# One core, expert stage of a two-block layer: the last 128 tokens' expert rows fetched by indirect DMA and multiplied on VectorE, TensorE's products 384 tokens wide

## The reference

```
def peer_ffn(h, w_q, sub_keys, u, v):        # blocks of 128 tokens, 8 heads, 128 keys, top 16
    q = (hx @ w_q).reshape(TOKEN_BLOCK, PEER_HEADS, 2, PEER_HALF)
    s = jnp.einsum('nhpd,hpkd->nhpk', q, sub_keys)
    ...                                      # top 16 of each half, top 16 of their 256 sums
    expert = (i1 * N_KEYS + i2).reshape(TOKEN_BLOCK, PEER_HEADS * PEER_TOPK)
    gate = jax.nn.softmax(best_s, axis=-1)
    u_sel = u[expert]                        # [128 tokens, 128 experts, 1024]
    v_sel = v[expert]
    act = jax.nn.gelu(jnp.einsum('nd,ned->ne', hx, u_sel), approximate=False)
    return jnp.einsum('ne,ned->nd', gate * act, v_sel)
```

## Time and profile before

| | us |
|---|---|
| three timed runs | 2605.48, 2605.72, 2604.08; median 2605.48 |
| profiled execution | 2603.68, its span 2601.9 |
| TensorE busy | 2467.9 (95%), 12856 matmuls |
| GpSimd busy | 1559.2 (60%) |
| VectorE busy | 1405.7 (54%) |
| ScalarE busy | 585.3 (22%) |
| DMA | 375.41 MB, mean 144 GB/s |
| matmuls of the experts and other weights from `hT` / of the down product (line 683) | 1055.8 / 667.4 busy |

### The profile page before, as it was taken

The page is one execution under the profiler, slowest core; times in us unless marked ns, Lnnn a source line. Parts: engine busy times, 40 slices in busy tenths (PEclk is TensorE's granted clock), DMA queues, the critical chain, the costliest instruction groups (busy, mean ns, idle before and its releaser), DMA issues.

```text
span 2601.9 us, 37796 instructions
## 1 busy us (share of the span) xinstructions
PE 2467.9 (95%) x12856; PEld 1258.8 (48%) x12856; DVE 1405.7 (54%) x2431; ACT 585.3 (22%) x1194; POOL 1559.2 (60%) x1048
## 2 busy tenths in 40 slices
PE   6879989999999999999999999999899898999997
PEld 3435534444555555434444444444357544457743
DVE  6996748998677777229722222240204533564434
ACT  2112211111222222111111111110126332245412
POOL 6764459888766766799866666560570166830063
PEclk8989999999999999999999999999999999999999
DMA  6224443555447857877755655560220022210021
GB/s 261 92 79 156 142 164 122 149 154 150 141 147 237 257 153 238 264 258 269 247 203 200 206 198 208 198 217 13 82 97 1 9 89 89 97 49 1 9 73 49
DMA packets 189247, 375.41 MB, mean 144 GB/s; under 512 B 13536, under 2 KB 79200, under 8 KB 189152
## 3 DMA queue, kind: packets, MB, share of 16 engines
q1 hardware_dynamic: 119696, 332.64, 38.2%
q10 hardware_dynamic: 69456, 41.50, 5.4%
HBM read 302.78 MB, written 71.30 MB: 144 GB/s over the span
## 4 chain that ended last, share of the span: by engine, by line
PE 83%; POOL 2%; DVE 2%; issue 1%; ACT 1%; DMA 0%; DVEq 0%; SPq 0%; POOLq 0%; ACTq 0%
PE ps L683 68%; PE ps L820 4%; PE ps L841 4%; PE ps L829 2%; PE ps L953 2%; PE ps L764 1%; POOL arena L653 1%; POOL parts L635 1%; DVE ps L1337 1%; ACT arena L1091 0%; POOL ring L633 0%; POOL arena L651 0%; DVE arena L1370 0%; PE ps L812 0%; PE ps L1053 0%
## 5 line engine op out<-in xcount | busy, mean ns | idle before, releaser
L683 PE MATMUL ps<-hT,parts 128*128 128x512 f16 x4800 | 1055.8, 380 | 38.2 <-DVE arena L1371 14.1
L632 POOL TENSOR_SCALAR parts<-ring 128x1024 f16<-128x1024 f32 x261 | 289.0, 1107 | 809.4 <-PE ps L683 784.1
L683 PEld LDWEIGHTS ps<-hT,parts 128*128 128x128 f16 x4800 | 467.0, 98 | 597.7 <-issue 22.3
L683 PE MATMUL ps<-arena 128*128 128x512 f16 x3072 | 667.4, 380 | 6.7 <-DVE arena L1734 6.7
L635 POOL TENSOR_TENSOR parts<-ring,parts 128x1024 f16<-128x1024 f32 x261 | 568.8, 2179 | 21.8
L683 PEld LDWEIGHTS ps<-arena 128*128 128x128 f16 x3072 | 301.2, 98 | 373.7 <-issue 14.8
L1729 DVE TENSOR_TENSOR arena<-arena 128x512 f32<-128x512 f32 x128 | 143.6, 1122 | 432.7 <-DMA arena<-gate_mem 430.2
L653 POOL TENSOR_TENSOR arena<-ring,arena 128x1024 f16<-128x1024 f32 x128 | 283.0, 2211 | 10.7
L633 POOL TENSOR_SCALAR ring<-ring 128x1024 f32<-128x1024 f32 x261 | 282.0, 1081 | 0.0
L651 POOL TENSOR_SCALAR arena<-ring 128x1024 f16<-128x1024 f32 x128 | 147.7, 1154 | 170.3 <-PE ps L683 170.3
L1202 ACT ACTIVATE spare<-ps 128x512 f32<-128x512 f32 x128 | 76.5, 597 | 567.5 <-PE ps L683 419.2
(11 more groups left out here) (172 smaller groups left out, 2270.2 us busy)
## 6 DMA issues: line engine op xcount, KB each, us to landing
ring<-w SPq DMA_DIRECT2D x133, 512.0 KB, 3.3
ring<-u SPq DMA_DIRECT2D x128, 512.0 KB, 3.9
ring<-v SPq DMA_DIRECT2D x128, 512.0 KB, 3.4
act_mem<-spare SPq DMA_DIRECT2D x128, 256.0 KB, 4.0
gate_mem<-arena ACTq DMA_DIRECT2D x4, 8192.0 KB, 42.7
arena<-act_mem SPq DMA_DIRECT2D x128, 256.0 KB, 3.6
arena<-gate_mem SPq DMA_DIRECT2D x128, 256.0 KB, 3.9
arena<-ada_w SPq DMA_DIRECT2D x48, 512.0 KB, 6.4
```

Of the source, the lines that this page charges most:

```text
L632: G.tensor_scalar(dst[:, 0, :], src, WS, 1.0, ALU.mult, ALU.mult).then_inc(scaled, 1)
L683: ins = [T.matmul(out_, a, b, start=start and j == 0, stop=stop and j == 2) for j, (a, b) in enumerate(((lhs[0], rhs[0]), (lhs[0], rhs[1]) ...
```

## The change

1. **384 tokens dense, 128 fetched.** `FEW` = 128 tokens (the last block) leave the dense products: `up`, gates, gelu, activations and gates in DRAM, `multiply` and `down_chunk` are 384 wide (`DENSE`), gate groups 48 instead of 64, gate blocks four of 96 tokens instead of four of 128.
2. **Their rows.** For expert slot k of 128, an indirect DMA from GpSimd brings row `expert[token, k]` of `u` to each token's partition (128 x 4 KB), into one of six buffers (`ROWS_AHEAD`). VectorE forms the dot product with the token's `h` (turned into PSUM by TensorE). One gelu, one product with the gates, then the same 128 fetches from `v`, and VectorE adds them up weighted, in the down loop. TensorE folds the sum into the last 128 columns of the banks.
3. **Who cuts.** From chunk 100 of the up product (`RAISED`) ScalarE makes the high half and the scaled tile (`raise_tile`), GpSimd only the low half. In the down product ScalarE makes all high halves of `v` (`v_tile_high`), eight chunks ahead.
4. **Loops.** GpSimd's and VectorE's down loops and ScalarE's are written out. SyncE's down loop is as before; the v tiles 4 to 7 are loaded later, after the activation stores.
5. **Norms of q and k.** ScalarE makes the squares while it copies and scales most rows; VectorE's share shrinks; the gains are applied by feature after the transposes.

The diff, cut to its core:

```diff
-BATCH = 128
+FEW = 128
+DENSE = S - FEW
+BATCH = DENSE // 4
+GROUPS = DENSE // GROUP
+ROWS_AHEAD = 6
+PER_TILE = 4
+V_LEAD = 8
+FETCH = AT_GATES + GROUP
+RAISED = AT_GATES + GROUPS + RING
...
+        def few_chunk(k):
+            return 2 + 112 * k // FEW
...
 SyncE
-                sp.dma_start(tile_of(act_mem, c), gelu[:, r % 2, :]).then_inc(act_out[r % 2], 16)
+                sp.dma_start(tile_of(act_mem, c), gelu[:, r % 2, 0:DENSE]).then_inc(act_out[r % 2], 16)
...
             for c in range(TAIL, CHUNKS):
-                load(S_V + c - TAIL, v_in[c - TAIL])
+                if c - TAIL < RING:
+                    load(S_V + c - TAIL, v_in[c - TAIL])
                 store_act(c, c)
...
-            for c in range(4):
-                load(S_V + GROUP + c, v_in[GROUP + c])
+            for c in range(RING, GROUP + 4):
+                load(S_V + c, v_in[c])
...
 GpSimd
+            def cut_raised(n):
+                pool.wait_ge(raised, 2 * (n - T_EXP - RAISED + 1))
+                src, dst = ring[:, n % RING, :], parts[:, n % RING, :, :]
+                G.tensor_tensor(dst[:, 1, :], src, dst[:, 0, :], ALU.subtract).then_inc(parts_ready, 1)
+
+            def fetch(n):
+                if n >= ROWS_AHEAD:
+                    wait_apart(rows_used, n - ROWS_AHEAD + 1)
+                rows = u_rows_in if n < FEW else v_in.rearrange("c p n -> (c p) n")
+                at = n % FEW
+                G.indirect_dma_start(
+                    out=fetched_rows[:, n % ROWS_AHEAD, :], out_offset=None, in_=rows,
+                    in_offset=bass.IndirectOffsetOnAxis(ap=few_idx[:, at:at + 1].bitcast(U32), axis=0),
+                ).then_inc(rows_fetched[n % ROWS_AHEAD], 16)
...
             def cut_v(c, it=0):
...
-                wait_apart(loaded[(S_V + c) % RING], it * 64 + 16 * ((S_V + c) // RING + 1))
-                G.tensor_scalar(dst[:, 0, :], src, 1.0, 1.0, ALU.mult, ALU.mult).then_inc(v_high, 1)
                 pool.wait_ge(v_high, it * 2 * GROUP + (c + 1))
                 G.tensor_tensor(dst[:, 1, :], src, dst[:, 0, :], ALU.subtract).then_inc(parts_ready, 1)
...
+            cut_tiles(RING, T_EXP + FETCH, 0)
+            pool.wait_ge(pick_loaded, 16 * 2 * SIDES)
+            for n in range(ROWS_AHEAD):
+                fetch(n)
+            cut_tiles(T_EXP + FETCH, T_EXP + RAISED, 0)
+            n = ROWS_AHEAD
+            for c in range(RAISED, CHUNKS):
+                for _ in range(PER_TILE):
+                    if n < FEW:
+                        fetch(n)
+                        n += 1
+                cut_raised(T_EXP + c)
+            while n < FEW + ROWS_AHEAD:
+                fetch(n)
+                n += 1
...
+            for c in range(CHUNKS):
+                while n < 2 * FEW and few_chunk(n - FEW) <= c:
+                    fetch(n)
+                    n += 1
                 cut_v(c)
...
 TensorE
-            ups(AT_GATES + 4, AT_GATES + S // GROUP, 4)
-            ups(AT_GATES + S // GROUP, CHUNKS)
+            ups(AT_GATES + 4, AT_GATES + GROUPS, 4)
+            for k in range(KC):
+                for side in range(SIDES):
+                    for j, half in enumerate(hr(k)):
+                        mm = T.matmul(ps[side * FEW:(side + 1) * FEW, 4 + k // 4, (k % 4) * P:(k % 4 + 1) * P],
+                                      half[:, DENSE:S], ident_h, start=(j == 0), stop=(j == 1))
+            mm.then_inc(few_turned, 1)
+            ups(AT_GATES + GROUPS, CHUNKS)
             pe.wait_ge(gelu_ready, CHUNKS)
+            pe.wait_ge(rows_used, FEW)
...
-                last.then_inc(down, 1)
+                T.matmul(ps[:, o, DENSE:S], few_sum[:, o * P:(o + 1) * P], fold, start=True,
+                         stop=True).then_inc(down, 1)
...
 ScalarE
+            def raise_tile(n):
+                act.wait_ge(loaded[n % RING], 16 * (n // RING + 1))
+                src = ring[:, n % RING, :]
+                A.activation(parts[:, n % RING, 0, :], src, ACT.Copy, scale=WS).then_inc(raised, 1)
+                A.activation(src, src, ACT.Copy, scale=WS).then_inc(raised, 1)
+
+            for c in range(AT_GATES + GROUPS, CHUNKS):
+                gelu_chunk(c % 4, c)
+                if RAISED <= c + RING - 1 < CHUNKS:
+                    raise_tile(T_EXP + c + RING - 1)
+            act.wait_ge(rows_used, FEW)
+            A.activation(few_dot, few_dot, ACT.Gelu).then_inc(few_gelu, 1)
...
+            def v_tile_high(c):
+                if c >= 2 * GROUP:
+                    act.wait_ge(down, c - 2 * GROUP + 1)
+                act.wait_ge(loaded[(S_V + c) % RING], 16 * ((S_V + c) // RING + 1))
+                A.activation(v_parts[:, c % (2 * GROUP), 0, :], ring[:, (S_V + c) % RING, :],
+                             ACT.Copy).then_inc(v_high, 1)
...
+            for c in range(V_LEAD):
+                v_tile_high(c)
+            for c in range(CHUNKS):
+                high(c % (2 * GROUP), c)
+                if c + V_LEAD < CHUNKS:
+                    v_tile_high(c + V_LEAD)
...
 VectorE
+            for k in range(FEW):
+                row = await_rows(k)
+                V.tensor_tensor_reduce(out=row, in0=row, in1=few_h, scale=1.0, scalar=0.0, op0=ALU.mult,
+                                       op1=ALU.add, accum_out=few_dot[:, k:k + 1]).then_inc(rows_used, 1)
...
+            def add_few(k):
+                row = await_rows(FEW + k)
+                w = few_dot[:, k:k + 1]
+                dve.wait_ge(rows_used, FEW + k)
+                if k == 0:
+                    dve.wait_ge(down, 1)
+                    V.tensor_scalar(few_sum, row, w, None, ALU.mult).then_inc(rows_used, 1)
+                else:
+                    V.scalar_tensor_tensor(out=few_sum, in0=row, scalar=w, in1=few_sum, op0=ALU.mult,
+                                           op1=ALU.add).then_inc(rows_used, 1)
+
+            k = 0
+            for c in range(CHUNKS):
+                multiply(c % (2 * GROUP), c, c // (2 * GROUP))
                 if c >= 1:
-                    low_part(c - 1, c - 1)
+                    low_part((c - 1) % (2 * GROUP), c - 1)
+                if c == 2:
+                    dve.wait_ge(few_gelu, 1)
+                    own.link(V.tensor_tensor(few_dot, few_dot, few_gate, ALU.mult))
+                while k < FEW and few_chunk(k) <= c:
+                    add_few(k)
+                    k += 1
```

More of the change, by code:

```diff
@@ L239, in build @@
         chosen = cut(NT, 3, P)
+        pick_f = cut(P)
+        pick_row = cut(P)
         zsum = cut(16)
         peer_qT = cut(PH, S)
+        assert cut.at <= ROOM
         cut = Cut()
@@ L992, in down_chunk @@
                     lhs, rhs = down_parts(at, o)
-                    first, last = three(ps[:, o, :], lhs, rhs, isinstance(c, int) and c == 0, False)
+                    first, last = three(ps[:, o, 0:DENSE], lhs, rhs, isinstance(c, int) and c == 0, False)
                 last.then_inc(down, 1)
@@ L1483, in _ @@
-            for i in range(NT):
-                dve.wait_ge(took["act"], count_taken("kvi", i))
-                own.do(V.tensor_tensor(scr[:, 0, 0:HD], tr[:, i, 0:HD], tr[:, i, 0:HD], ALU.mult))
-                own.link(V.tensor_tensor(scr[:, 0, HD:2 * HD], tr[:, i, 2 * HD:3 * HD], tr[:, i, 2 * HD:3 * HD], ALU.mult))
-                own.link(V.tensor_reduce(stat[:, i * 10 + 8:i * 10 + 10],
-                                         scr[:, 0, 0:2 * HD].rearrange("p (h d) -> p h d", d=HD), AX, ALU.add),
-                         stat_ready if i == NT - 1 else None)
@@ L1490, in _ @@
-            dve.wait_ge(root_ready, 1)
-            own.link(V.reciprocal(stat2[:, 0:40], stat2[:, 0:40]))
-            for i in range(NT):
+                dve.wait_ge(q_squares, i + 1)
+                own.do(V.tensor_reduce(stat[:, i * 10:i * 10 + 8], mask[:, i, :].rearrange("p (h d) -> p h d", d=HD),
+                                       AX, ALU.add), stat_ready if i == NT - 1 else None)
+            dve.wait_ge(root_ready, 1)
+            own.link(V.reciprocal(stat2[:, 0:40], stat2[:, 0:40]), rates)
@@ L1500, in _ @@
-                own.settle()
-            for b, (a, g) in enumerate(((0, "g_k"), (2 * HD, "g_ik"))):
-                for i in range(NT):
-                    two = dup[:, b, i, :].rearrange("p (t d) -> p t d", t=2)
-                    src = tr[:, i, a:a + HD].unsqueeze(1).broadcast_to([P, 2, HD])
-                    own.link(V.scalar_tensor_tensor(out=two, in0=src, scalar=stat2[:, i * 10 + 8 + b:i * 10 + 9 + b],
-                                                    in1=g_row(g, 2), op0=ALU.mult, op1=ALU.mult),
-                             tok_ready if i == NT - 1 else None)
+                own.do(V.tensor_tensor(q3, q3, rs, ALU.mult), tok_ready)
```

197 lines of the change are left out of this document (127 added, 70 removed).

## The result

The changed kernel takes **3214.33 us** (median of 4 runs, 3209.79 to 3222.57) against 2605.57 before (4 runs, 2604.08 to 2605.72): ratio 1.234, 95% interval 1.2327 to 1.2356. The forecast was 3118, range 2850 to 3340.

What follows compares the result with a forecast made beforehand. TensorE bounds the expert products before; rings of waits after. First part -3, tiles to 48 -13, gates -54, fetch stage +144, down +438: +512 on 2603.7, 3116; timed runs 1.8 above, 3118; range 2850 to 3340.

Steps and rivals of the forecast that it cites:

- fetch stage: Up tiles 96 to 127 and TensorE's start of the down product: 328 us instead of 184, +144.
- down stage: Down product: 1116 us instead of 678, +438, with 105 chunks at 9.6 us each.
- First part: q and k norms: TensorE's 6.52 us wait goes, ScalarE's added passes cost; net -3 us, bounds -6.5 and +2.
- Tiles to 48: Up tiles 0 to 47: router holds ScalarE at tile 40, then 3.9 us a tile; 662 instead of 675.
- Gates: Up tiles 48 to 95: VectorE's one-hot products become the bound, 4.93 us a group; tile 96 at 899 instead of 966.
- Up ring: Up tiles 100 to 127: cut, issues, landing, gelu and raising passes close a ring over one tile, 10.5 us a tile.
- Down ring: Down product: next pair waits, through v load, cut and row fetch, for this chunk's add; 10.6 us, 9.6 a chunk.
- Clock: TensorE's granted clock in the down product expected low, at no cost: 7.8 us at 1.2 GHz hide under 9.6.
- Signs: Down product: v loads 9-11 us apart, VectorE idling 6 a chunk, TensorE under half busy; two new waits among the longest.
- Rival A: Down product: rings have slack and throughput decides, 4.4 us a chunk, total 2500; chance 0.10.
- Rival B: GpSimd takes over 3 us for 128 addresses: fetch tiles +97, down product +210, total 3425; chance 0.08.
- Rival C: Gate block stores in 384 B runs take 85 us, ScalarE stands 26 us twice, total 3170; chance 0.08.

Runs made afterwards that it cites:

- run 4: Changed kernel with each of the 128 fetched addresses giving 64 columns (256 B) instead of 1024 (4 KB), last 128 tokens' expert output left out: 3140.3 us.
- run 8: Changed kernel without row fetches, their products and sums (last 128 tokens' expert output left out), 384-wide matmuls kept: 2476.0 us.
- run 9: On run 7's kernel, ScalarE raises v tile c+4 instead of c+8, and x's way back starts at chunk 96 instead of 0: 2480.05 us, ratio 0.952.
- run 1: Changed kernel with SyncE loading the pair ahead of the v tile in the down loop: 2805.5 us.
- run 2: Changed kernel with SyncE issuing the activation store ahead of the u tile load in the up loop: 3115.1 us.
- run 7: Kernel with SyncE loading pair c, then v tile c+4, store ahead of u tile; first pairs behind last store, first v tiles raised and cut earlier: 2548.7 us.

## Why the prediction was right, step by step

The forecast is 96 us under the measured 3214, of a loss of 609. The spans differ by 610.4 us. By stage:

| | forecast | measured |
|---|---|---|
| up to the first gates (680.4 before) | -16 | -15.0 |
| gates, 48 groups | 4.93 a group | 4.88 a group |
| gates done, tile 96 begins (966 before) | 899 | 899.5 |
| fetch stage | 328 (+144) | 353 (+169) |
| down stage | 1116 (+438) | 1183 (+506) |
| behind the experts | 0 | +1.8 |

The two large stages were both forecast too short, so the agreement does not come from errors that cancel.

- **First part.** The transposes start at 87.71, without idle time, in place of 92.13: -4.4 against -3.
- **Tiles to 48.** The sum was right and one reason was not. The exps began at 625.31 and not at 634.6: in the trace of before it was ScalarE that came late to them, not the router. TensorE stood 23.74 us until 627.80, and then the transposes waited for the gate products until 641.5, which the forecast had at 642.7; five tiles later came the first gates, 665.4 against 664.4. (Before, the router was ready at 622.4 and ScalarE came to the exps at 634.6.)
- **Gates.** VectorE bounds as worked out; its idle time of 1.14 a group is gone:

```profile
865.37 1.22 DVE L1831 TENSOR_TENSOR xT<-xT,ps 128x1024 f16<-128x1024 f16 x1
```

- **Up ring.** 10.8 against 10.5; a raising pass is 1.05 against 1.1; cut 127 began at 1205.7, forecast 1196. (The terms of this ring, as the prediction lists them, add to 9.9 and not to 9.7; with its 0.8 for company that is 10.7.) Mis-sized were the last ten rows: they came every 1.8 us and not 1.4, the last product ended at 1232.4 instead of 1211, and TensorE started 20 us later instead of 16. The forecast counted the rows' own bytes there. The engines were indeed full (404 GB/s from 1212 to 1232 us), but they also moved stores and pairs. By queue, packets, MB and share (q0 is GpSimd's, the rows):

```profile
q0 software_dynamic: 1620, 5.92, 74.1%
q1 hardware_dynamic: 1576, 2.15, 29.1%
```

  So 2.15 of 8.07 MB were not the rows'. With the rows' bytes gone (run 4) the last products follow each other every 1.14 us, VectorE's own pace.
- **Down ring.** This is the largest miss in size: the stage came 67 us longer than forecast, of 96 in all. The v loads show it: between 1340 and 2335 us six of seven gaps are 11.3 us on average against the 10.6 of the forecast, the seventh 3.25 against 3.3, so a chunk takes 10.2 in place of 9.6. The ordinary turn by terms, forecast behind it: the link from the end of the cut to the multiply 4.75 (4.9), multiply to the end of the add 2.22 (2.34), from there to the start of the fetch 0.81 (0.2 for all semaphores of the ring), issue and gap 0.97 (1.0), cut 2.13 (2.13 and 0.1 for a gap); 10.88 in all (the forecast's terms add to 10.7). So the term that was mis-sized is the hand-over from VectorE to GpSimd. The link was right at the median, with the 0.35 that the forecast took off for narrower pairs; its longer turns (5.54 in the first one shown, up to 7.0) make the rest, and the rows' bytes have a share in them, since the mean turn of run 4 is 0.3 shorter.
- **Clock.** The granted clock was 0.78 at 1260 to 1660, low as expected, at no cost: TensorE waited anyway. In runs 8 and 9, with 400 and 369 us of work in 400, it was 1.00 and 0.99.
- **Signs.** Both new waits are among the longest, the v loads come 11 us apart, and GpSimd's cut waits for ScalarE in tiles 100 to 127 (101 us in all). Two signs were off: VectorE idles some 9 us ahead of an ordinary multiply and not 6 (the ring less its own 2.2), and TensorE is busy 56% of the down stage (223.7 of 400 us), not under half.
- **Rival A** (throughput decides) was wrong for this order. Its price for a kernel without rings, 4.4 a chunk and 2500, is close to run 9's 4.47 and 2480; the totals agree in part by luck, as run 9 also began the down stage 26 us earlier than A has it and had it 7 us longer. **Rival B** falls by one row of the changed kernel:

```profile
L687 POOL DMA_INDIRECT arena<-u_rows,spare x128 | 120.6, 942 | 37.6 <-issue 28.7
```

- **Rival C** falls by its landing time, 36.4 us for a block where 85 was feared:

```profile
gate_mem<-arena ACTq DMA_DIRECT2D x4, 6144.0 KB, 36.4
```

The Trainium skill (DMA: Bandwidth & Descriptors, Specifications) has stores under 512 B fall below full rate; here a block in runs of 384 B landed in 36.4 us, the same number of runs of 512 B in 42.7 before. That is 15% less time for 25% fewer bytes, so 12% less a second, and nothing like the doubling that was feared.

**Where the gain went.** The narrow matmuls are worth 128 us as they stand (run 8, with the rest of the change but the rows, and with an up ring still in them). With the rows and better orders the kernel takes about as long (run 9, 2480). That does not make the rows free: the down stage is 572 us with them and 510 without, and the earlier start of run 9 hides it. A kernel without rows in the orders of run 9 was not run. The order of the changed kernel costs 734 us against that (3214 to 2480): 409 by one pair of lines and 99 by another, 10 of which both count, 154 by the two-chunk ring that is left then, and 83 by the order on ScalarE's and GpSimd's queues at the start and in the lead of the v tiles (with the places of the first pairs and of x's way back, which were not tried apart).

Not settled: why the two-chunk ring of run 1 takes 12.7 us for its two chunks on average (13.3 where shown), where the one-chunk ring takes 10.2 for its one (the stretched add is 2.4 of it in the chunk shown, and not every chunk has it). The eighteen microseconds that a store took at the end of the up stage in run 2 are settled in part: there it stood behind four pairs on SyncE's queue, and gelu waited 15.66 us; in run 7, with the pairs behind the last store, it waited 1.25. How full engines share their time between the queues is not shown.

## What to carry to other kernels

When a change adds a wait, follow the new edge round through every in-order queue until it comes back to itself. If it does, add up the durations, divide by the number of iterations that the loop spans, and compare that with the bound of the stage: a ring that spans one iteration costs its full latency each time, and one more buffer or two lines exchanged on a queue let it span two. Don't count on half: here the stage fell by 34 to 36%, and in run 1 engines that used to take turns got in each other's way. Before giving up a change whose trace shows everybody half busy, look at the loads that stand in front of other loads on the queue that issues them.

## What the hardware showed that was not expected

- From the end of VectorE's add to the start of GpSimd's indirect fetch 0.8 us pass (1717.62 to 1718.43; 0.80 to 0.83 in all 56 plain turns), four times what the forecast gave for it. GpSimd's own semaphore step (`wait_apart`) lies in between; no run shows how much of it that is. Back-to-back indirect issues stand 0.3 us apart.
- An indirect fetch of 128 rows is one instruction of 0.94 us on GpSimd whether each row gives 4 KB or 256 B (run 4); with the engines full the transfers moved 400 GB/s in all (run 2).
- The same VectorE operation is 0.55 us alone and 2.48 us beside a GpSimd cut, and a kernel freed of its rings pays this in the engine that then bounds.
